# Full-width matmuls in a triangular solve, and table masks shared between three engines, in a hybrid RWKV-7 and PEER layer

## What is computed

```python
# the time mixing: per head a 64x64 state, run forwards and backwards over the tokens
sa = einsum('bhvk,bhk->bhv', s, -kk_t)
s = s * w_t + sa[..., None] * (kk_t * a_t) + v_t[..., None] * k_t
y = einsum('bhvk,bhk->bhv', s, r_t)
...
# the PEER mixer: each token picks 8 x 16 experts out of 16384, idx and gates per slot
act = gelu(einsum('nd,nhkd->nhk', x, expert_u[idx]))
out = einsum('nhk,nhkd->nd', act * gates, expert_v[idx])
```

## Time and profile before

| | |
|---|---|
| median of 3 runs | 3564.57 us (3540.98 to 3569.79) |
| the profiled execution | 3564.57 us, of which its span is 3562.8 us |
| PE busy | 3103.0 us (87%) |
| DVE busy | 2444.3 us (69%) |
| ACT busy | 1465.5 us (41%) |
| POOL busy | 721.2 us (20%) |
| granted TensorE clock, mean | 0.946 |

### The profile page before, as it was taken

One profiled execution on the slowest core, in us unless ns is written; L12 is line 12 of the kernel. 1 busy time (PEld: TensorE's weight loads), 2 busy tenths in 40 slices (PEclk: granted clock), 3 DMA queues, 4 the chain that ended last, 5 costly groups with the idle time before them and its releaser, 6 DMA issues.

```text
span 3562.8 us, 57659 instructions
## 1 busy us (share of the span) xinstructions
PE 3103.0 (87%) x21864; PEld 2673.4 (75%) x21864; DVE 2444.3 (69%) x3113; ACT 1465.5 (41%) x1891; POOL 721.2 (20%) x387
## 2 busy tenths in 40 slices
PE   6987998957888889496998777779999799999997
PEld 2336998945766777495998777779999687787776
DVE  5995553256455554535798877757777699899997
ACT  6884332324333343435333555433333333333333
POOL 0000000001001101201565322211111234334431
PEclk9998999978999999798999888899999899999999
DMA  9992332300000000132444788999999999999996
GB/s 378 420 392 106 130 127 108 119 12 5 6 7 5 5 5 3 60 125 99 139 151 162 273 301 300 304 340 360 357 359 379 399 417 417 417 417 417 417 417 258
DMA packets 207434, 811.62 MB, mean 228 GB/s; under 512 B 81472, under 2 KB 101056, under 8 KB 118336
## 3 DMA queue, kind: packets, MB, share of 16 engines
q1 hardware_dynamic: 170432, 541.14, 40.9%
q0 software_dynamic: 36864, 268.45, 18.7%
HBM read 769.16 MB, written 40.37 MB: 227 GB/s over the span
## 4 chain that ended last, share of the span: by engine, by line
DMA 26%; PE 11%; DVE 9%; ACT 4%; issue 3%; SPq 1%; POOL 0%; DVEq 0%; ACTq 0%
DMA work<-act_table 11%; DMA raw<-expert_u 10%; DMA x<-u_rows,idx 4%; DVE wlo L2097 2%; ACT whi L1754 2%; DVE x L2055 2%; PE ps L1559 1%; PE ps L1560 1%; PE ps L1561 1%; DVE work L2132 1%; DVE wlo L2137 1%; PE ps L1816 1%; PE ps L1818 1%; PE ps L1817 1%; PE ps L1909 1%
## 5 line engine op out<-in xcount | busy, mean ns | idle before, releaser
L1559 PE MATMUL ps<-hhi,whi 128*128 128x256 f32 x2048 | 594.5, 290 | 60.0 <-DVE wlo L1548 27.5
L1560 PE MATMUL ps<-hlo,whi 128*128 128x256 f32 x2048 | 584.4, 285 | 0.0
L1561 PE MATMUL ps<-hhi,wlo 128*128 128x256 f32 x2048 | 584.0, 285 | 0.0
L1559 PEld LDWEIGHTS ps<-hhi,whi 128*128 128x128 f32 x2048 | 398.2, 194 | 72.9 <-issue 32.5
L1909 PE MATMUL ps<-whi,hhi 128*128 128x512 f32 x1024 | 402.9, 393 | 36.1 <-DVE hlo L2115 18.7
L282 PE MATMUL ps<-hhi,whi 128*128 128x384 f32 x1056 | 357.1, 338 | 79.2 <-DVE hlo L1416 42.9
L1910 PE MATMUL ps<-wlo,hhi 128*128 128x512 f32 x1024 | 400.0, 391 | 0.0
L1911 PE MATMUL ps<-whi,hlo 128*128 128x512 f32 x1024 | 399.7, 390 | 0.0
L1560 PEld LDWEIGHTS ps<-hlo,whi 128*128 128x128 f32 x2048 | 398.5, 195 | 0.0
L1561 PEld LDWEIGHTS ps<-hhi,wlo 128*128 128x128 f32 x2048 | 397.9, 194 | 0.0
L1942 POOL DMA_INDIRECT work<-expert_v,idx x128 | 286.9, 2241 | 440.0 <-DVE work L2132 423.9
(11 more groups left out here) (298 smaller groups left out, 6159.7 us busy)
## 6 DMA issues: line engine op xcount, KB each, us to landing
raw<-expert_u SPq DMA_DIRECT2D x128, 1024.0 KB, 7.7
z<-w_ada SPq DMA_DIRECT2D x72, 1024.0 KB, 15.4
raw<-expert_v SPq DMA_DIRECT2D x64, 1024.0 KB, 15.0
work<-expert_v SPq DMA_DIRECT2D x64, 1024.0 KB, 14.8
raw<-w_in SPq DMA_DIRECT2D x50, 1024.0 KB, 4.8
raw<-w_ada SPq DMA_DIRECT2D x24, 1024.0 KB, 14.5
raw<-w_out SPq DMA_DIRECT2D x16, 1024.0 KB, 4.8
raw<-w_query SPq DMA_DIRECT2D x16, 1024.0 KB, 5.0
```

The lines of the kernel that those rows point to most:

```text
L1559: pe.matmul(bank, whi[:, r, k, :], moving_hi, start=(k == 0), stop=False)
L1560: pe.matmul(bank, whi[:, r, k, :], moving_lo, start=False, stop=False)
L1561: last = pe.matmul(bank, wlo[:, r, k, :], moving_hi, start=False, stop=(k == KD - 1))
```

## The change

Two things are changed. In the scan stage the x product and the t product are no longer cut in halves: one matmul with 128 stationary columns writes what two with 64 wrote. In the table stage the multiplication by the gates is divided: ACT does the first two tokens of each quad as before, POOL the other two in one instruction of 128x256. The subtractions `low_of` of the blocks M_SCAT, M_SCAT + 1 and M_SCAT + 2i + 3 go to POOL, those of M_SCAT + 2i + 2 stay on DVE. POOL now has a program order in which its gathers stand behind these, and the three gathers of an iteration behind its `gate_two(q + 3)`. On DVE `mask(0)` and `mask(1)` come after the first four dots.

```diff
-                            for rows_ in heads:
-                                last = pe.matmul(ps[rows_, g % 2, i * HEAD:(i + 1) * HEAD].rearrange("p (n b) -> p n b", b=b),
-                                                 G[:, g, i, 0, rows_], early(tn[:, g, i], g, b)[:, 0], start=True, stop=True)
+                            last = pe.matmul(ps[:, g % 2, i * HEAD:(i + 1) * HEAD].rearrange("p (n b) -> p n b", b=b),
+                                             G[:, g, i, 0, :], early(tn[:, g, i], g, b)[:, 0], start=True, stop=True)
...
-                                for rows_ in heads:
-                                    last = pe.matmul(ps[rows_, 2 + g % 2, i * HEAD:(i + 1) * HEAD], tt[:, g, i, rows_], xl[:, g, i],
-                                                     start=True, stop=True)
+                                last = pe.matmul(ps[:, 2 + g % 2, i * HEAD:(i + 1) * HEAD], tt[:, g, i], xl[:, g, i], start=True, stop=True)
...
-                def gate_quad(q):
+                def gate_two(q):
                     act.wait_ge(fa_mask.sem, q + 1)
-                    for t in range(4):
+                    for t in range(2):
...
                     for t in range(4):
-                        pe.wait_ge(fa_act.sem, 4 * q + t + 1)
+                        if t < 2:
+                            pe.wait_ge(fa_act.sem, 2 * q + t + 1)
+                        elif t == 2:
+                            pe.wait_ge(fa_pool.sem, q + 1)
...
-                for s in range(FIRST_DOTS, SLOTS):
+                low_of(pool, nc.gpsimd, M_SCAT)
+                low_of(pool, nc.gpsimd, M_SCAT + 1)
+                pool.wait_ge(slots_here.sem, 1)
+
+                def gate_two(q):
+                    pool.wait_ge(fa_mask.sem, q + 1)
+                    a = (4 * q) % 8 + 2
+                    f = fa[:, a:a + 2, :]
+                    nc.gpsimd.tensor_tensor(
+                        f, f, slot[:, 0, 4 * q + 2:4 * q + 4].rearrange("p (t o) -> p t o", o=1).to_broadcast([P, 2, NK]),
+                        ALU.mult).then_inc(fa_pool.sem, 1)
+
+                gate_two(0)
+                gate_two(1)
+                s = FIRST_DOTS
+                for i in range(SCAT):
+                    q = QUADS * i
+                    gate_two(q + 2)
+                    gate_two(q + 3)
+                    for _ in range(SCAT_DOTS):
+                        gather_u(s)
+                        s += 1
+                    if i < SCAT - 1:
+                        gate_two(q + 4)
+                        gate_two(q + 5)
+                    low_of(pool, nc.gpsimd, M_SCAT + 2 * i + 3)
+                while s < SLOTS:
                     gather_u(s)
+                    s += 1
...
-                low_of(dve, nc.vector, M_SCAT)
-                mask(0)
-                mask(1)
                 for s in range(FIRST_DOTS):
                     dot(s)
                 s = FIRST_DOTS
+                mask(0)
+                mask(1)
                 for i in range(SCAT):
                     q = QUADS * i
                     mask(q + 2)
                     mask(q + 3)
-                    dot(s)
-                    low_of(dve, nc.vector, M_SCAT + 2 * i + 1)
-                    for n in range(1, SCAT_DOTS - 1):
-                        dot(s + n)
+                    for n in range(SCAT_DOTS - 1):
+                        dot(s)
+                        s += 1
                     low_of(dve, nc.vector, M_SCAT + 2 * i + 2)
                     if i < SCAT - 1:
                         mask(q + 4)
                         mask(q + 5)
-                    dot(s + SCAT_DOTS - 1)
-                    s += SCAT_DOTS
-                low_of(dve, nc.vector, M_REST + 1)
+                    dot(s)
+                    s += 1
```

More of the change, by code:

```diff
@@ L1531, in build_program @@
         slots_turned, slots_here = sem("slots_turned"), sem("slots_here")
-        fa_mask, fb_mask, fa_act = sem("fa_mask"), sem("fb_mask"), sem("fa_act")
+        fa_mask, fb_mask, fa_act, fa_pool = sem("fa_mask"), sem("fb_mask"), sem("fa_act"), sem("fa_pool")
         table_done, staged = sem("table_done"), sem("staged")
@@ L1724, in copies @@
                                          ACT.Copy).then_inc(staged.sem, 1)
-                gate_quad(0)
-                gate_quad(1)
+                gate_two(0)
+                gate_two(1)
                 for i in range(SCAT):
@@ L1731, in _ @@
                     copies(q + 1)
-                    gate_quad(q + 2)
-                    gate_quad(q + 3)
+                    gate_two(q + 2)
+                    gate_two(q + 3)
                     gelu(m, g)
@@ L1738, in _ @@
                     if i < SCAT - 1:
-                        gate_quad(q + 4)
-                        gate_quad(q + 5)
+                        gate_two(q + 4)
+                        gate_two(q + 5)
                     gelu(m + 1, g + 1)
```

## The result

| | before | after |
|---|---|---|
| median of 4 runs | 3556.89 us (3540.98 to 3569.79) | 3714.47 us (3701.62 to 3724.95) |
| ratio, 95% interval | | 1.0444 [1.0384, 1.0503] |
| the profiled execution (span) | 3564.57 us (3562.8) | 3716.84 us (3715.0) |
| granted TensorE clock, mean | 0.946 | 0.930 |

The change makes the kernel 4.4% slower. The profiled executions differ by 152.2 us in span, and the traces divide them up. "Iteration 0" and "15" are counted at their first masks.

A forecast was written before the change was run, and what follows sets the result against it. PE, with DVE by turns, was taken to bound the scan, and a ring of waits through gathers and dots the table stage. 3564.6 + 33 (scan) + 137 (table stage) gave 3735 us; range 3640 to 3790 us.

The forecast's parts named there:

- Part A, a level, +0.6 us: Scan: with wide matmuls 0.111 us apart and shape-change gaps gone, a level costs 0.6 us more than 6.23 us.
- 8 x 4.1: Scan: each of eight passes grows by 4.1 us, together +33 us.
- Part B, the order: Table stage: the first gather stands behind gates awaiting the mask just ahead of its dot, so every iteration waits a whole gather.
- the ring: Table stage: a dot frees a buffer, POOL issues the next gather, it lands, the next dot; 18.2 us before, 28.0 predicted.
- Part B, exclusion: Table stage: DVE's dots, masks and subtractions never overlap POOL's elementwise work; period 28.0 us with it, 22.2 without.
- My rival without exclusion: Table stage: POOL and DVE overlap, period 22.2 us, +40 us for the stage, 3638 us in all; chance 0.12.
- Part B, the period, 28.0 us: Table stage: one iteration's lock and ring pieces sum to 28.2, taken as 28.0 us; 15 iterations make 420 us.
- Part B, the stores, 10 us each: Table stage: three gate-table stores cost 10 us each instead of 15, as longer iterations give raw loads more time; 30 us.
- Prologue +4, end 0: Ahead of the table loop POOL's two subtractions for DVE's one add 4 us; behind it the last store hides POOL's subtraction.
- Unchanged period (3598): Table stage: the period stays because POOL's gates run early enough, leaving only the scan's +33; 3598 us, chance 0.05.
- gaps that stay (3789): Scan: gaps ahead of x products stay though the array shape no longer changes; 3735 + 54 = 3789 us, chance 0.07.
- cheap wide matmuls (3644): Scan: wide matmuls cost only their 64 moving columns, -58 us for the stage instead of +33; 3644 us, chance 0.08.

The follow-up runs named there:

- a_x_wide: Kernel before with only the scan's x products made full width, in all passes, t products in halves, table stage unchanged; 3557.19 us, ratio 0.9977.
- a_t_wide: Kernel before with only the scan's t products made full width, in all passes, x products in halves, table stage unchanged; 3568.90 us, ratio 1.0006.
- order_only: Kernel before with one added wait: POOL issues an iteration's first gather only after its fourth mask; no arithmetic moved; 3603.13 us, ratio 1.0117.
- b_ahead: As b_only, but POOL issues the first two gathers of each iteration one iteration earlier; 3590.51 us, ratio 1.0086 to the kernel before.
- b_gathers_first: As b_only, but on POOL the first two gathers of an iteration stand ahead of its gates; 3647.84 us, ratio 1.0234 to the kernel before.
- b_lows_only: Kernel before with only the table stage's subtractions changed, every second one on POOL behind its iteration's gathers, gates on ACT; 3662.51 us, ratio 1.0246.
- b_ahead_blank: As b_ahead, with POOL's subtraction in the loop replaced by writing zeros, reading nothing; 3535.63 us, ratio 0.9932 to the kernel before.
- b_only: Kernel before with only the table-stage part of the change, scan as before; 3667.69 us, ratio 1.0286.

## Why the prediction was right, point by point

The forecast was 3735 us with a range of 3640 to 3790; the median is 3714.47. The mechanism held for the larger part, the table stage. That the sum came out so close is in part luck: the scan cost 13.7 us more than I had (46.7 for 33), the table stage with its two ends 32 us less (105.4 for 137), and within the scan two things that I had left out met, some 23 us gained and some 37 lost. The kernel before also has a median of 3556.89 us now, 7.7 below the 3564.57 that I added to, so the change is 157.6 us for the 170 of the sum.

**Part A, a level, +0.6 us: right in kind, a little too much.** A level costs 0.49 us more (6.72 - 6.23). The loads are 0.11 us apart, and the gap ahead of an x product is gone with the wide form alone, which a_x_wide and a_t_wide show. The first pass, where nothing else changed, grew by 4.7 us for the 4.1 I had.

**Part A, "8 x 4.1": this step failed.** I took eight equal passes at an unchanged clock. The middle ones didn't grow: 4.1 us of longer levels met 3.9 us that the start of a pass gives back, where the pause with its instruction loads is gone and the short stretch at the 1.2 GHz level with it. The earlier trace rows had the sign of it, a mean clock of 0.95 in a stage where PE is busy 88% of the time, and I didn't ask where the low clock stood. Passes two to seven took 470.0 us against 468.7, +1.3 for the +24.6 predicted. The eighth pass took 40.7 us more for 4.1, at the low clock for some 75 us. Together 4.7 + 1.3 + 40.7 = 46.7 us for 33. I had named the low clock only for the table stage, as something that would come from PE being idle; it came in the scan, where PE was busiest.

**Part B, the order: right, but with too narrow a reason.** The whole gather in the open is what the change costs; order_only shows it with no work moved, and b_ahead takes most of the cost away with all the work moved. I named the gates' place as the cause. b_gathers_first and b_lows_only show that POOL's subtraction closes the ring as well, and harder.

**Part B, exclusion: right.** Masks of 0.68 us took up to 5.14 in the changed kernel, a dot 9.10 us in the prologue, where two subtractions of POOL stood against it. b_ahead_blank fits POOL's reading as what locks: an operation of POOL that reads nothing lay across masks and held none up. What the moved arithmetic costs with the gathers free, exclusion included, is about 25 us of the 110 (b_ahead); the rest is order. The 25 are not the price of exclusion alone, as DVE's missing subtraction is in them with the other sign. My rival without exclusion put it at 97 us, since it also let POOL's ring run free; the two terms can't be read off one by one from a ring.

**Part B, the period, 28.0 us: 26.9.** By its pieces: the lock fell on the masks instead of on the third dot, 6.7 us for masks and subtraction together, where I had 4.6 for the subtraction and then 3.9 for masks and gates (two gates hold the four masks up by 0.41 us, 2.90 for 2.49, and the dot behind them by as much, 2.70 for 2.29; I had 1.46 for the two). The second gather's 7.7 us took the place of my 5.9 for the first, 2.2 for its dot and 0.8 of wait.

**Part B, the stores, 10 us each: 5.** From first gather to first gather, the three iterations with a store take 32.3, 31.9 and 32.2 us, the plain ones 26.3 to 27.8. The reasoning (a raw load in a longer iteration has more slack) was right and didn't go far enough. Together, iterations 0 to 15 cost +98.3 for +133: the period made 15 x 1.1 = 17 us of the difference and the stores 14, and iteration 0 took 22.8 us instead of a full period, 4.

**Prologue +4, end 0:** +5.8 and +1.3, of which 4.2 lie between the ready indices and iteration 0.

**The rivals.** Unchanged period (3598) is refuted by b_only, gaps that stay (3789) by a_t_wide beside a_x_wide, and cheap wide matmuls (3644) by the 0.11 us and the 6.72 us of a level. No exclusion (3638) is refuted by the masks and by the time. What I had named as signs came but for one: 1152 loads at each of the two lines, no gap, a wait of 6.2 us for the first gather (10.0 with a store), stretched masks and a dot, masks every 26.9 us. The middle passes stayed at 78.4 us where I had said 82, and that was the sign of the step that failed.

## What to carry to other kernels

Before an instruction with a wait is put into a queue that also issues transfers, follow every instruction behind it once around the ring. Here a single wait ahead of one gather, with no work moved, cost at least about as much (1.2%) as all of the moved work with the gathers kept free (0.9%; the intervals overlap). Moving elementwise work with two operands to POOL didn't relieve a DVE that works on two SBUF operands: they took turns, and POOL took 4.6 us where DVE took 2.3. In a stage that PE bounds, read the idle time and the granted clock pass by pass: halving the number of matmuls took a pause at the start of six passes away (some -23 us, 3 of them the low clock behind it) and brought the low clock to the last pass (some +37 us), where the matmuls by themselves were put at +33.

## What the runs showed of the hardware that I had not expected

- With the x and the t products at full width and no front steps between, PE stood at the 1.2 GHz level for some 75 us (0.50 from 1395 to 1470, PE busy 10.00 of 10 us). It fell there right behind a pause (busy 3.34 of 5 us), which didn't bring the clock down in the kernel before, and came back with PE still busy at full width on other products. Either product in halves leaves a mean of 0.93 to 0.95 for that pass. In passes two to seven, with the same wide products and front steps in between (PE busy 94%), the clock was 1.00. What exactly the chip reacts to stays open: a_x_wide and a_t_wide differ from the changed kernel both in the share of PE's busy time and in the columns that work, and no run holds one of them fixed.
- A loop of 857 matmuls a pass (and as many weight loads) had 9 packets on the instruction queue and a gap of 4.4 us on PE in every pass, followed by some microseconds at the low clock; loops of 714 and 570 had none and gaps of 1.0 us.
- An operation on POOL that writes and doesn't read held up no mask; the subtraction, which reads, made a mask of 0.68 us last up to 5.14 us in the changed kernel and 6.62 us in b_ahead.
